# Swapping the rotary channel halves with DMAs inside SBUF instead of a TensorE permutation, and turning at the end of each block's VectorE list

## The chip, the cores and the metric

One Trainium2 chip, of which the kernel uses one core. The metric is the device time in microseconds (us) of one execution of the whole program. Engines are named as in the profile: PE is TensorE, DVE is VectorE, ACT is ScalarE, POOL is GpSimd, SP is SyncE.

## What is computed

Two layers of a hybrid mixer on 256 latent and 256 context tokens of width 2048. Each layer has one input projection whose columns form a convolution branch, a two-directional gated recurrence, and windowed attention with 8 query and 2 key heads of 128 channels; then one output projection. The latent queries and keys get a two-dimensional rotary turn before attention:

```
def _rotate_half(t):
    t1, t2 = jnp.split(t, 2, axis=-1)
    return jnp.concatenate([-t2, t1], axis=-1)

def apply_axial_rope(x, cos, sin):
    xf = x.astype(jnp.float32)
    xr, xc = jnp.split(xf, 2, axis=-1)
    xrot = jnp.concatenate([_rotate_half(xr), _rotate_half(xc)], axis=-1)
    return (xf * cos[:, None, :] + xrot * sin[:, None, :]).astype(x.dtype)
```

So with the 128 channels of a head on the partitions, the four groups of 32 channels change places in pairs (0 with 1, 2 with 3), and the first of each pair gets a minus. That is done for 10 tiles of 128 channels x 256 tokens a layer (2 k, 8 q), 20 in all.

## The kernel before

Channels lie on the 128 partitions, tokens in the free dimension. A layer is a list of blocks of 128 output columns each (`BLOCKS`, 56 a layer: x, k, v, the convolution's inputs, then q 0-3, their gates, q 4-7, their gates, two further gate groups, 16 output blocks). The program's l counts the layers from 0; this text says layer 1 (l = 0) and layer 2 (l = 1). A block's weights (1 MB) are split into a high and a low fp32r part: ACT copies the high half (`hi`), DVE subtracts for the low (`lo`), in two halves of 8 tiles each, and PE does three products per tile (L614 to L616), 16 tiles a block. In layer 1 a block streams 512 columns, in layer 2 most blocks stream only 256.

Everything around these products is written out as a table of steps: step b of an engine's loop does block b's part and the side work tied to b. The order on each engine is the order in the code:

- PE, step b: `mm_half(b, 0)`; transposes of the modulation rows (`ada_tp`, L509) and P times V (`pv`) where they fall due; `mm_half(b, 1)`; `rope_mm`; value transposes; recurrence gates (`lru_mm`, L648); attention scores (L669); probability transposes (`p_tp`, L682); modulation products (`ada_mm`, L501).
- ACT, step b: `hi` of the block two ahead, each half after PE has finished with the buffer (that is the halves of block b); the block's copy out of PSUM (`evac`, L875 for q); square roots and tanh of the recurrence; the rest of attention; `ada_rows` (L813), which copies modulation sums into `adasb`, the same memory as `lnr`, and first waits for the latest turn.
- DVE, step b: `lo` of the block two ahead (L1077), `evac`, `rope`, the running maximum of the softmax (L1299), the recurrence's scans and taps (L1249 to L1234), the convolution's taps (L1272, L1276: `CONV_TAPS`), `att_norm` (L1309, L1311).
- POOL has ten memsets and nothing else. SP issues all DMAs.

The rotary turn of block r stands in step `ROPE_AT[l]`: step 9 and 10 for k of layer 1, 13 and 14 for k of layer 2, and in both layers steps 17 to 20 for q 0-3 (blocks 16 to 19) and 25 to 28 for q 4-7 (blocks 24 to 27). PE multiplies a signed permutation matrix (`perm`, fp32) with the tile (L627); DVE multiplies the PSUM result with sine into `lnr` (L1211), the tile with cosine in place (L1212), and adds (L1214). `misc` lists who holds the PSUM bank `psM`: the next user on PE waits for the last (`misc_free`), so a `rope_mm` waits until DVE has read the one before.

Who waits for a turn: `scores` of each layer's first group (step 22) for the second k and q 3; the first group of the second key head for q 7 (step 30 in layer 1, step 29 in layer 2: `LAST_GROUPS`); `ada_rows` in steps 14 and 27 of layer 1.

```
ROPE_AT = [{9: 4, 10: 5, 17: 16, 18: 17, 19: 18, 20: 19, 25: 24, 26: 25, 27: 26, 28: 27},
           {13: 12, 14: 13, 17: 16, 18: 17, 19: 18, 20: 19, 25: 24, 26: 25, 27: 26, 28: 27}]
```

Of the kernel before, what the change touches and what calls it, by code (L numbers as in the profile page):

```python
# [21 lines left out]
ALU = mybir.AluOpType  # L22
AX = mybir.AxisListType

P = 128
D = 2048
DT = D // P
LAT, CTX = 256, 256
# [9 lines left out]
CT = 4  # L38
EPS = 1e-6
ADA_KINDS = 3  # L40
SHIFT, SCL, GATE = range(3)
# [10 lines left out]
BLOCKS = [[("x", t) for t in range(CT)] + first + REST for first in (KV + GLU, GLU + KV)]  # L52
# [159 lines left out]
def program(nc, io, known):  # L212
    ctx = ExitStack()
    with ctx:
# [180 lines left out]
        def conv_taps(l, b):  # L395

            plan = CONV_TAPS[l]
            assert sum(plan) == TAPS * CT // 2
            if not 0 <= b - CONV_AT[l] < len(plan):
                return []  # L400
            first = sum(plan[:b - CONV_AT[l]])
            return [(2 * (n // TAPS) + i, n % TAPS) for n in range(first, first + plan[b - CONV_AT[l]]) for i in range(2)]

        block = ctx.enter_context(nc.Block())

# [64 lines left out]

        @block.gpsimd
        def _(pool):
            nc.gpsimd.memset(cstat[:, :, :], 0.0).then_inc(*C.up("cstat_zero"))
            nc.gpsimd.memset(eps[:, :], EPS).then_inc(*C.up("eps_set"))
            nc.gpsimd.memset(bd[:, :, :, :], 0.0).then_inc(*C.up("bd_zero"))
            for l in range(LAYERS):
                if l:
                    pool.wait_ge(*C.at("scores", l - 1, max(groups(l - 1))))
                else:  # L480
                    pool.wait_ge(*used(last_of(NRAW + 1)))
                    pool.wait_ge(*used(last_of(NRAW + 2)))
                nc.gpsimd.memset(lrux[:, :, :, :], 0.0).then_inc(*C.up("lrux_zero", l))
                if l == 0:
                    pool.wait_ge(*used(last_of(NRAW)))
                    nc.gpsimd.memset(glu[:, :, :, :], 0.0).then_inc(*C.up("glu_zero"))

        @block.tensor
        def _(pe):  # L490
# [105 lines left out]
            def mm_half(gb, j):  # L596
# [18 lines left out]
                    mm(ps[:, 0:n], hi, hl[:, k, t], start=False, stop=False)  # L615
                    last = mm(ps[:, 0:n], lo, hh[:, k, t], start=False, stop=(at == DT - 1))  # L616
                last.then_inc(*C.up("mm", u))

            def rope_mm(l, b):

                kind, i = BLOCKS[l][b]
                if not misc:
                    pe.wait_ge(*C.at("evac_act", OPEN[0] - 1))
                pe.wait_ge(*C.at("evac_act", l * NB + b))
                misc_free(l)
                src = kT[:, i, 0:LAT] if kind == "k" else q[:, i, 0:LAT]
                mm(psM[:, 0:LAT], perm, src, start=True, stop=True).then_inc(*C.up("rope_mm", l, kind, i))  # L627

            def misc_free(l):

                if misc:
                    pe.wait_ge(*C.at(*misc[-1]))
# [105 lines left out]
            for gb in range(GLOB):  # L738
                l, b = divmod(gb, NB)
                if b == 0:  # L740
                    scores_free.clear()
                    if l:
                        rms_mm(l)
                        for a in PLAN[NB]:
                            ada_mm(*a)
                        for quarter in range(4):
                            for pair in range(SIDE // 2):
                                mm_quarter(quarter, pair)
                    else:
                        for c in range(CHUNKS):  # L750
                            mm_chunk(c)
                if b < OPEN[l]:
                    continue
                mm_half(gb, 0)

                for a in done_before(l, b):
                    ada_tp(*a)
                if b - TP_LAG[l] - 1 in groups(l):
                    pv(l, b - TP_LAG[l] - 1)
                mm_half(gb, 1)  # L760

                if b in ROPE_AT[l]:
                    rope_mm(l, ROPE_AT[l][b])
                    misc.append(("rope_t", l, *BLOCKS[l][ROPE_AT[l][b]]))
                if b and BLOCKS[l][b - 1][0] == "v":
                    i = BLOCKS[l][b - 1][1]
                    pe.wait_ge(*C.at("evac_act", gb - 1))
                    misc_free(l)
                    for kt in range(4):
                        last = nc.tensor.transpose(psM[:, kt * P:(kt + 1) * P], tbuf[:, kt * P:(kt + 1) * P], ident)  # L770
                    last.then_inc(*C.up("v_tp", l, i))
                    misc.append(("v_out", l, i))
                if b in LRU_MM[l]:
                    lru_mm(l, LRU_MM[l].index(b))
                if b in groups(l):
                    scores(l, b)
                if b - TP_LAG[l] in groups(l):
                    p_tp(l, b - TP_LAG[l])
                if b == LN_SUM[l]:
                    ln_mm(l, "ln_sum")  # L780
                if b == LN_VAR[l]:
                    ln_mm(l, "ln_var")
                if b == PW_AT:
                    for m in range(CT):
                        pw_mm(l, m)
                    misc.append(("pw_out", l, CT - 1))
                if l == 0:
                    for a in PLAN[b]:
                        ada_mm(*a)
# [271 lines left out]
        def _(dve):  # L1061
# [142 lines left out]
            def rope(l, b):  # L1204

                kind, i = BLOCKS[l][b]
                x = kT[:, i, 0:LAT] if kind == "k" else q[:, i, 0:LAT]
                dve.wait_ge(*C.at("rope_mm", l, kind, i))
                if (l, kind, i) != (0, "k", 0):
                    dve.wait_ge(*C.ago("rope"))  # L1210
                V.tensor_tensor(lnr[:, 0:LAT], psM[:, 0:LAT], sin, ALU.mult).then_inc(*C.up("rope_t", l, kind, i))  # L1211
                V.tensor_tensor(x, x, cos, ALU.mult).then_inc(*C.up("rope_c", l, kind, i))  # L1212
                dve.wait_ge(*C.ago("rope_c"))
                V.tensor_tensor(x, x, lnr[:, 0:LAT], ALU.add).then_inc(*C.up("rope", l, kind, i))  # L1214

            def taps(l, t):

# [118 lines left out]
            for dst, src, f in ((s4, tiny[:, 2, 0:n], 4.0), (s4n, tiny[:, 2, 0:n], -4.0), (dwh, at["dw_w"], 0.5),  # L1336
                                (hbr, at["b_r"], 0.5), (hbi, at["b_i"], 0.5), (lnhg, at["ln_g"], 0.5),
                                (lnhb, at["ln_b"], 0.5), (nsink, sink, -1.0)):
                V.tensor_scalar(dst, src, f, None, ALU.mult).then_inc(*C.up("derived"))
            dve.wait_ge(*C.ago("derived"))  # L1340

            for m in range(DT - 1):
                rms_add(0, m)
            for gb in range(GLOB):
# [28 lines left out]
                if gb + 2 < GLOB and b < NB - 1:  # L1373
                    lo(unit(0, gb + 2, 1))
                evac(gb)
                if b in ROPE_AT[l]:
                    rope(l, ROPE_AT[l][b])
                if b in groups(l):
                    att_max(l, b)
                if b in LRU_MM[l]:  # L1380
# [3 lines left out]
                if b in LRU_TAPS[l]:  # L1384
                    taps(l, LRU_TAPS[l].index(b))
                conv(l, conv_taps(l, b))
                if b in groups(l):
                    att_norm(l, b)
                if b == LN_SUM[l] - 1:
# [104 lines left out]
```

## Time and profile before

| | |
|---|---|
| time, median of 3 runs | 1322.59 us (1319.38 to 1323.63) |
| the profiled execution: time | 1322.9 us |
| its span in the trace | 1321.1 us, at a mean granted PE clock of 0.99 |
| PE busy | 1258.6 us (95%) |
| DVE busy | 733.7 us (56%) |
| ACT busy | 534.6 us (40%) |
| POOL busy | 8.2 us (1%) |
| HBM read | 230.54 MB, 176 GB/s over the span |

The busy time of an engine says how much work it has, not whether that work sets the end. For that the chain of waits is read, and then the stretch itself in the timeline: start, duration, engine, line, and in brackets how long the engine sat idle before it and what released it. PE's matmuls are pipelined, so the durations in the timeline overlap; what one costs is seen from start to start.

### The profile page before, as it was taken

How to read it: one execution, taken by the hardware profiler on the slowest of the kernel's cores; microseconds unless marked ns; L12 is line 12 of the kernel's file. 1: busy time of each engine (PE TensorE's matmuls, PEld its weight loads, DVE VectorE, ACT ScalarE, POOL GpSimd, SP SyncE). 2: the span in 40 equal slices, each digit the busy share in tenths (PEclk: the TensorE clock that was granted, in tenths of full speed). 3: DMA queues.
4: the chain of work that ended last, by engine and by line, in shares of the span. 5: the costliest groups of instructions: out<-in, count | busy, mean ns of one | idle time of the engine just before them, and what ended most of it. 6: DMA issues, size and time to landing. Idle time of an engine off the chain costs nothing.

```text
span 1321.1 us, 17033 instructions
## 1 busy us (share of the span) xinstructions
PE 1258.6 (95%) x7004; PEld 970.9 (73%) x7004; DVE 733.7 (56%) x1188; ACT 534.6 (40%) x843; POOL 8.2 (1%) x10
## 2 busy tenths in 40 slices
PE   3798999999999999999999999989999999999996
PEld 1465777767777777776777777758887998889995
DVE  3443436687565555552343233385789976755554
ACT  5222344452223334453332122244665554565452
POOL 0000100000000000000000000000000000000000
PEclk9999999999999999999999999989999999999998
DMA  9999655446443333333454554453332433325541
GB/s 343 332 320 324 220 201 212 191 192 263 155 187 128 128 127 127 128 128 134 169 225 175 213 208 173 186 191 104 120 131 93 160 128 128 128 96 192 182 169 64
DMA packets 76317, 233.73 MB, mean 177 GB/s; under 512 B 8016, under 2 KB 50128, under 8 KB 54352
## 3 DMA queue, kind: packets, MB, share of 16 engines
q1 hardware_dynamic: 76240, 232.65, 49.0%
q8 instruction: 55, 0.90, 0.3%
q14 instruction: 22, 0.18, 0.0%
HBM read 230.54 MB, written 2.10 MB: 176 GB/s over the span
## 4 chain that ended last, share of the span: by engine, by line
PE 83%; DVE 7%; DMA 5%; ACT 3%; issue 1%; SPq 0%; DVEq 0%; ACTq 0%
PE psum_block L614 21%; PE psum_block L615 20%; PE psum_block L616 20%; PE psum_ada L501 5%; PE psum_scores L691 3%; PE psum_scores L648 2%; PE psum_scores L669 2%; DMA raw<-in_w_ada 2%; DVE w_lo L1077 2%; DMA Y<-in_xT 1%; PE psum_scores L682 1%; DMA qreg<-in_w_ada 1%; DVE T L1128 1%; DVE h_lo L1135 1%; DMA glu<-in_w_ada 1%
## 5 line engine op out<-in xcount | busy, mean ns | idle before, releaser
L614 PE MATMUL psum_block<-h_hi,w_hi 128*128 128x512 f32 (+1 forms) x1616 | 562.4, 348 | 0.7 <-ACT glu L1050 0.7
L615 PE MATMUL psum_block<-h_lo,w_hi 128*128 128x512 f32 (+1 forms) x1616 | 547.9, 339 | 0.0
L616 PE MATMUL psum_block<-h_hi,w_lo 128*128 128x512 f32 (+1 forms) x1616 | 547.7, 339 | 0.0
L1077 DVE TENSOR_TENSOR w_lo<-raw,w_hi 128x1024 fp32r<-128x1024 f32 x218 | 263.4, 1218 | 398.6 <-ACT w_hi L803 398.4
L803 ACT ACTIVATE w_hi<-raw 128x1024 fp32r<-128x1024 f32 x218 | 228.5, 1053 | 530.1 <-PE psum_block L616 516.2
L614 PEld LDWEIGHTS psum_block<-h_hi,w_hi 128*128 128x128 f32 x1616 | 306.3, 190 | 78.1 <-issue 38.7
L615 PEld LDWEIGHTS psum_block<-h_lo,w_hi 128*128 128x128 f32 x1616 | 306.6, 190 | 35.3 <-issue 3.8
L616 PEld LDWEIGHTS psum_block<-h_hi,w_lo 128*128 128x128 f32 x1616 | 306.4, 190 | 34.2
L1276 DVE SCALAR_TENSOR_TENSOR Y<-glu,small,Y 128x512 f32<-128x512 f32 (+1 forms) x240 | 130.4, 612 | 0.0
L501 PE MATMUL psum_ada<-raw,cstat 128*32 128x512 f32 x512 | 67.2, 616 | 5.4 <-DMA raw<-in_w_ada 5.4
L917 ACT ACTIVATE T<-psum_scores,stats 128x512 f32<-128x512 f32 (+1 forms) x48 | 28.9, 615 | 52.7 <-DVE stats L1301 52.7
L844 ACT ACTIVATE h_hi<-T,ada 128x256 fp32r<-128x256 f32 x64 | 28.7, 501 | 45.4 <-DVE T L1128 45.4
L1085 DVE TENSOR_REDUCE tiny<-psum_ada 128x4 f32<-128x16 f32 x16 | 2.0, 169 | 71.3 <-PE psum_ada L531 71.3
L523 PE MATMUL psum_ada<-raw,cstat 128*32 128x256 f32 x272 | 20.5, 424 | 21.1 <-DMA raw<-in_w_ada 21.1
L691 PE MATMUL psum_scores<-T,v 128*128 128x512 f32 x80 | 36.4, 593 | 1.4 <-ACT T L932 1.4
L501 PEld LDWEIGHTS psum_ada<-raw,cstat 128*32 128x32 f32 x512 | 11.5, 109 | 34.5 <-issue 26.5
L831 ACT ACTIVATE T<-Y 128x512 f32<-128x512 f32 (+1 forms) x48 | 26.1, 550 | 22.4 <-DVE Y L1201 13.3
L648 PE MATMUL psum_scores<-T,bd 128*128 128x512 f32 x64 | 30.7, 625 | 3.9 <-DVE T L1234 3.9
L923 ACT ACTIVATE T<-T,stats 128x512 f32<-128x512 f32 (+1 forms) x48 | 27.3, 640 | 13.6 <-DVE stats L1311 13.6
L1234 DVE SCALAR_TENSOR_TENSOR T<-qreg,small,T 128x512 f32<-128x512 f32 x48 | 32.5, 745 | 0.0
L523 PEld LDWEIGHTS psum_ada<-raw,cstat 128*32 128x32 f32 x272 | 7.7, 118 | 32.5 <-issue 16.1
L669 PE MATMUL psum_scores<-kT,qreg 128*128 128x512 f32 x64 | 31.4, 611 | 0.0
(174 smaller groups left out, 1105.6 us busy)
## 6 DMA issues: line engine op xcount, KB each, us to landing
raw<-in_w_blocks SPq DMA_DIRECT2D x105, 1024.0 KB, 4.8
raw<-in_w_ada SPq DMA_DIRECT2D x81, 1024.0 KB, 5.5
qreg<-in_w_ada SPq DMA_DIRECT2D x10, 1024.0 KB, 11.2
glu<-in_w_ada SPq DMA_DIRECT2D x5, 1024.0 KB, 9.7
Y<-in_xT SPq DMA_DIRECT2D x4, 1024.0 KB, 12.4
T<-in_xT SPq DMA_DIRECT2D x16, 256.0 KB, 7.2
raw<-in_w_blocks SPq DMA_DIRECT2D x4, 896.0 KB, 11.4
raw<-in_pw SPq DMA_DIRECT2D x2, 1024.0 KB, 6.2
```

The source lines that it names most:

```text
L501: last = mm(psA[32 * j:32 * j + 32, :], cstat[:, k, 2:34], w[:, j * TOK:(j + 1) * TOK], start=(k == 0), stop=(k == DT - 1), tile_position= ...
L614: mm(ps[:, 0:n], hi, hh[:, k, t], start=(at == 0), stop=False)
L615: mm(ps[:, 0:n], hi, hl[:, k, t], start=False, stop=False)
L616: last = mm(ps[:, 0:n], lo, hh[:, k, t], start=False, stop=(at == DT - 1))
L648: last = mm(psS[:, 2 * d + g, :], bd[:, g, d * CT + t, :], T[:, 4 * d, :], start=True, stop=True)
L669: mm(psS[:, g, :], qt, kT[:, kv, :], start=True, stop=False)
L691: last = mm(psS[:, 0, :], v[:, kt, kv * HD:(kv + 1) * HD], T[:, 4 + kt, :], start=(kt == first), stop=(kt == 3))
L803: fn(wh[:, u % 4, 0:cols.stop - cols.start], raw_of(item)[:, cols], ACT.Copy).then_inc(*C.up("hi", u))
L917: fn(T[:, g, k0:TOK], psS[:, g, k0:TOK], ACT.Exp, scale=SCALE, bias=st[:, 1, g:g + 1], accum_out=st[:, 2, g:g + 1]).then_inc(*C.up("att_ex ...
L1077: V.tensor_tensor(wl[:, u % 4, 0:n], raw_of(item)[:, cols], wh[:, u % 4, 0:n].bitcast(F32), ALU.subtract).then_inc(*C.up("lo", u))
L1234: stt(out, x, lcw[:, c, k:k + 1], out, ALU.mult, ALU.add).then_inc(*C.up("taps", l, t, d))
L1276: stt(out, x, dwh[:, c:c + 1], out, ALU.mult, ALU.add).then_inc(*C.up("conv", l, t, k))
```

## The change

The permutation matmul goes. In its place POOL issues four DMAs for each turn, from SBUF to SBUF, 32 partitions of 1 KB each, that lay the tile's groups of 32 channels swapped into one of two halves of `lnr`. Each set of four waits for the tile's copy out of PSUM, and for the turn two before (whose half of `lnr` it uses); in layer 1 also for the modulation transposes that read `adasb`. DVE then multiplies the swapped copy with sine in place. The minus sign moves into the sine table: two small DVE instructions at the start of the program (the row sums of `perm`, and a scaling of `sin`). In DVE's list of a step, `rope` moves from ahead of the softmax maximum, recurrence and convolution to behind the convolution, ahead of `att_norm`. The users of `psM` no longer wait for turns.

```
+        def rope_of(l, b):
+            kind, i = BLOCKS[l][b]
+            return kT[:, i, 0:LAT] if kind == "k" else q[:, i, 0:LAT]
+
+        def turned_of(l, b):
+
+            n = list(ROPE_AT[l].values()).index(b) % 2
+            return lnr[:, n * LAT:(n + 1) * LAT]
...
         @block.gpsimd
         def _(pool):
+            def turn(l, s, b):
+
+                kind, i = BLOCKS[l][b]
+                order = list(ROPE_AT[l].values())
+                n = order.index(b)
+                pool.wait_ge(*C.at("evac_act", l * NB + b))
+                if n >= 2:
+                    pool.wait_ge(*C.at("rope", l, *BLOCKS[l][order[n - 2]]))
+                elif l:
+                    pool.wait_ge(*C.at("ln_n", 0, CT - 1))
+                    pool.wait_ge(*C.at("ada_tp", 1, GATE))
+                if l == 0:
+                    for step, items in PLAN.items():
+                        for rows in items:
+                            if step < s and rows[2] == DT - 1:
+                                pool.wait_ge(*C.at("ada_tp", *rows[:2]))
+                for quad in range(0, P, 32):
+                    nc.gpsimd.dma_start(turned_of(l, b)[quad:quad + 32, :], rope_of(l, b)[quad ^ 32:(quad ^ 32) + 32, :]
+                                        ).then_inc(*C.up(f"turned{n % 2}", l, kind, i, quad, by=16))
+
...
+                for s, b in ROPE_AT[l].items():
+                    turn(l, s, b)
...
-            def rope_mm(l, b):
-
-                kind, i = BLOCKS[l][b]
-                if not misc:
-                    pe.wait_ge(*C.at("evac_act", OPEN[0] - 1))
-                pe.wait_ge(*C.at("evac_act", l * NB + b))
-                misc_free(l)
-                src = kT[:, i, 0:LAT] if kind == "k" else q[:, i, 0:LAT]
-                mm(psM[:, 0:LAT], perm, src, start=True, stop=True).then_inc(*C.up("rope_mm", l, kind, i))
-
...
-                if b in ROPE_AT[l]:
-                    rope_mm(l, ROPE_AT[l][b])
-                    misc.append(("rope_t", l, *BLOCKS[l][ROPE_AT[l][b]]))
...
-                dve.wait_ge(*C.at("rope_mm", l, kind, i))
-                if (l, kind, i) != (0, "k", 0):
-                    dve.wait_ge(*C.ago("rope"))
-                V.tensor_tensor(lnr[:, 0:LAT], psM[:, 0:LAT], sin, ALU.mult).then_inc(*C.up("rope_t", l, kind, i))
+                x = rope_of(l, b)
+                turned = turned_of(l, b)
+                n = list(ROPE_AT[l].values()).index(b)
+                dve.wait_ge(*C.at(f"turned{n % 2}", l, kind, i, P - 32))
+                V.tensor_tensor(turned, turned, sin, ALU.mult).then_inc(*C.up("rope_t", l, kind, i))
                 V.tensor_tensor(x, x, cos, ALU.mult).then_inc(*C.up("rope_c", l, kind, i))
+                dve.wait_ge(*C.ago("rope_t"))
                 dve.wait_ge(*C.ago("rope_c"))
-                V.tensor_tensor(x, x, lnr[:, 0:LAT], ALU.add).then_inc(*C.up("rope", l, kind, i))
+                V.tensor_tensor(x, x, turned, ALU.add).then_inc(*C.up("rope", l, kind, i))
...
+            V.tensor_reduce(st[:, 0, 0:1], perm, axis=AX.X, op=ALU.add).then_inc(*C.up("derived"))
+            dve.wait_ge(*C.ago("derived"))
+            V.tensor_scalar(sin, sin, st[:, 0, 0:1], -1.0, ALU.mult, ALU.mult).then_inc(*C.up("derived"))
...
                 evac(gb)
-                if b in ROPE_AT[l]:
-                    rope(l, ROPE_AT[l][b])
                 if b in groups(l):
                     att_max(l, b)
...
                 conv(l, conv_taps(l, b))
+                if b in ROPE_AT[l]:
+                    rope(l, ROPE_AT[l][b])
                 if b in groups(l):
                     att_norm(l, b)
```

The line numbers of the changed kernel are about 20 higher: L1077 becomes L1095, L1180 L1198, the turn's L1211, L1212, L1214 become L1229, L1230, L1233, the convolution's L1276 becomes L1295, and the scores' L669 L690.

DVE, layer 2, steps 27 and 28, from `lo` of the block two ahead on. Before:

```order
L1077 TENSOR_TENSOR w_lo<-raw,w_hi 128x1024 x2
L1211 TENSOR_TENSOR lnr<-psum_misc,small 128x256
L1212 TENSOR_TENSOR qreg<-qreg,small 128x256
L1214 TENSOR_TENSOR qreg<-qreg,lnr 128x256
L1276 SCALAR_TENSOR_TENSOR Y<-glu,small,Y 128x256 x6
L1077 TENSOR_TENSOR w_lo<-raw,w_hi 128x1024
L1318 SCALAR_TENSOR_TENSOR Y<-psum_scores,Y 128x4x128
L1077 TENSOR_TENSOR w_lo<-raw,w_hi 128x1024
L1180 SCALAR_TENSOR_TENSOR Y<-Y,psum_block 128x256
L1211 TENSOR_TENSOR lnr<-psum_misc,small 128x256
L1212 TENSOR_TENSOR qreg<-qreg,small 128x256
L1214 TENSOR_TENSOR qreg<-qreg,lnr 128x256
```

The same place with the change:

```order
L1095 TENSOR_TENSOR w_lo<-raw,w_hi 128x1024 x2
L1295 SCALAR_TENSOR_TENSOR Y<-glu,small,Y 128x256 x6
L1229 TENSOR_TENSOR lnr<-lnr,small 128x256
L1230 TENSOR_TENSOR qreg<-qreg,small 128x256
L1233 TENSOR_TENSOR qreg<-qreg,lnr 128x256
L1095 TENSOR_TENSOR w_lo<-raw,w_hi 128x1024
L1337 SCALAR_TENSOR_TENSOR Y<-psum_scores,Y 128x4x128
L1095 TENSOR_TENSOR w_lo<-raw,w_hi 128x1024
L1198 SCALAR_TENSOR_TENSOR Y<-Y,psum_block 128x256
L1295 SCALAR_TENSOR_TENSOR Y<-glu,small,Y 128x256 x6
L1229 TENSOR_TENSOR lnr<-lnr,small 128x256
L1230 TENSOR_TENSOR qreg<-qreg,small 128x256
```

The turn of a step now stands behind the six convolution taps of that step instead of ahead of them, and reads `lnr`, not PSUM.

POOL, the end of its list in layer 1 and in layer 2 (four of the DMAs make one turn):

```order
L500 DMA lnr<-kT 32x256 x8
L500 DMA lnr<-qreg 32x256 x32
L512 MEMSET qreg 128x2096
L500 DMA lnr<-kT 32x256 x8
L500 DMA lnr<-qreg 32x256 x32
```

Before, the one MEMSET was POOL's only instruction there; now 40 DMAs stand in its queue ahead of it and 40 behind it, in program order.

## Rows read from the trace of the kernel before

**Rows 1.** The page, parts 1 and 4: busy time; chain that ended last
```profile
PE 1258.6 (95%) x7004; PEld 970.9 (73%) x7004; DVE 733.7 (56%) x1188; ACT 534.6 (40%) x843; POOL 8.2 (1%) x10
...
PE 83%; DVE 7%; DMA 5%; ACT 3%; issue 1%; SPq 0%; DVEq 0%; ACTq 0%
```

**Rows 2.** PE timeline, layer 2, end of step 28: start us, us, engine, line
```profile
1121.89 0.28 PE L616 MATMUL psum_block<-h_hi,w_lo 128*128 128x256 f32 x1
1122.01 0.59 PE L627 MATMUL psum_misc<-qreg,small 128*128 128x256 f32 x2
1122.25 0.47 PE L614 MATMUL psum_block<-h_hi,w_hi 128*128 128x256 f32 x1
1122.56 0.28 PE L615 MATMUL psum_block<-h_lo,w_hi 128*128 128x256 f32 x1
1122.67 0.28 PE L616 MATMUL psum_block<-h_hi,w_lo 128*128 128x256 f32 x1
```

**Rows 3.** PE timeline, layer 1: a step with a turn, and one without
```profile
320.24 0.39 PE L616 MATMUL psum_block<-h_hi,w_lo 128*128 128x512 f32 x1
320.47 0.59 PE L627 MATMUL psum_misc<-qreg,small 128*128 128x256 f32 x2
320.99 0.64 PE L501 MATMUL psum_ada<-raw,cstat 128*32 128x512 f32 x4
...
371.37 0.39 PE L616 MATMUL psum_block<-h_hi,w_lo 128*128 128x512 f32 x1
371.69 0.64 PE L501 MATMUL psum_ada<-raw,cstat 128*32 128x512 f32 x4
```

**Rows 4.** PE's waits, whole span: line, releaser, us in total, times, longest
```profile
PE psum_scores L648 <- DVE T L1234: 3.9, 2, 2.8
...
PE psum_misc L627 <- DVE lnr L1211: 0.3, 1, 0.3
```

**Rows 5.** Timelines of ACT, DVE and PE, layer 2, steps 13 and 14
```profile
1000.33 1.15 ACT L908 ACTIVATE qreg<-qreg 128x512 f32<-128x512 f32 x2
...
1001.00 1.29 DVE L1249 TENSOR_TENSOR T<-T,qreg 128x512 f32<-128x512 f32 x2
...
1006.14 4.06 DVE L1234 SCALAR_TENSOR_TENSOR T<-qreg,small,T 128x512 f32<-128x512 f32 x6
...
1010.25 1.13 PE L648 MATMUL psum_scores<-T,bd 128*128 128x512 f32 x2 [1.09 <-DVE T L1234]
```

**Rows 6.** Timelines of DVE, ACT and PE, layer 1, steps 27 and 28
```profile
467.50 0.42 DVE L1211 TENSOR_TENSOR lnr<-psum_misc,small 128x256 f32<-128x256 f32 x1
...
468.28 0.43 DVE L1214 TENSOR_TENSOR qreg<-qreg,lnr 128x256 f32<-128x256 f32 x1
468.62 4.06 DVE L1276 SCALAR_TENSOR_TENSOR Y<-glu,small,Y 128x512 f32<-128x512 f32 x6
...
468.80 0.60 ACT L813 ACTIVATE lnr<-psum_ada 128x512 f32<-128x512 f32 x1 [0.90 <-DVE qreg L1214]
...
473.02 0.60 PE L509 MATMUL psum_ada<-rounded,lnr 128*128 128x128 f32 x4
```

**Rows 7.** DVE: `lo` in the page's part 5; timeline, layer 2, step 25
```profile
L1077 DVE TENSOR_TENSOR w_lo<-raw,w_hi 128x1024 fp32r<-128x1024 f32 x218 | 263.4, 1218 | 398.6 <-ACT w_hi L803 398.4
...
1103.77 0.16 DVE L1309 TENSOR_TENSOR stats<-stats 128x4 f32<-128x4 f32 x1 [1.96 <-ACT stats L920]
```

**Rows 8.** Timelines of DVE and PE, layer 2, steps 28 and 29
```profile
1124.83 0.42 DVE L1211 TENSOR_TENSOR lnr<-psum_misc,small 128x256 f32<-128x256 f32 x1
...
1125.62 0.42 DVE L1214 TENSOR_TENSOR qreg<-qreg,lnr 128x256 f32<-128x256 f32 x1
1125.96 2.46 DVE L1276 SCALAR_TENSOR_TENSOR Y<-glu,small,Y 128x256 f32<-128x256 f32 x6
...
1128.19 1.02 PE L669 MATMUL psum_scores<-kT,qreg 128*128 128x512 f32 x2
```

**Rows 9.** DVE timeline, start of the program
```profile
7.98 0.31 DVE L1339 TENSOR_SCALAR der<-small 128x8 f32<-128x8 f32 x3
13.80 5.47 DVE L1108 TENSOR_TENSOR T<-T 128x512 f32<-128x512 f32 x7 [5.51 <-ACT T L831]
```

**Rows 10.** Timelines, layer 2: copies of q 0 and q 6; first scores
```profile
1033.47 0.38 ACT L875 ACTIVATE qreg<-psum_block 128x256 f32<-128x256 f32 x1 [1.27 <-DVE Y L1263]
...
1067.56 1.02 PE L669 MATMUL psum_scores<-kT,qreg 128*128 128x512 f32 x2
...
1108.55 0.36 ACT L875 ACTIVATE qreg<-psum_block 128x256 f32<-128x256 f32 x1
```

**Rows 11.** DMA issues by line: count, KB each, median us to landing; SP timeline
```profile
raw<-in_w_blocks SPq DMA_DIRECT2D x105, 1024.0 KB, 4.8
...
out<-Y SPq DMA_DIRECT2D x4, 512.0 KB, 3.7
...
822.40 0.33 SPq L454 DMA_DIRECT2D raw<-in_w_ada  x1
822.77 0.43 SPq L454 DMA_DIRECT2D raw<-in_w_blocks  x1
```

More of the change, by code:

```diff
@@ L1206, in rope @@
                 kind, i = BLOCKS[l][b]
-                x = kT[:, i, 0:LAT] if kind == "k" else q[:, i, 0:LAT]
-                dve.wait_ge(*C.at("rope_mm", l, kind, i))
-                if (l, kind, i) != (0, "k", 0):
-                    dve.wait_ge(*C.ago("rope"))
-                V.tensor_tensor(lnr[:, 0:LAT], psM[:, 0:LAT], sin, ALU.mult).then_inc(*C.up("rope_t", l, kind, i))
+                x = rope_of(l, b)
[3 more added lines that the diff above has]
+                V.tensor_tensor(turned, turned, sin, ALU.mult).then_inc(*C.up("rope_t", l, kind, i))
                 V.tensor_tensor(x, x, cos, ALU.mult).then_inc(*C.up("rope_c", l, kind, i))
+                dve.wait_ge(*C.ago("rope_t"))
                 dve.wait_ge(*C.ago("rope_c"))
-                V.tensor_tensor(x, x, lnr[:, 0:LAT], ALU.add).then_inc(*C.up("rope", l, kind, i))
+                V.tensor_tensor(x, x, turned, ALU.add).then_inc(*C.up("rope", l, kind, i))
             def taps(l, t):
```

## The prediction

> **What bounds the kernel now.** I read the page first: PE is busy 95% of the span, and the chain that ended last runs 83% over PE and 7% over DVE [rows 1]. So an instruction taken off PE is worth its time unless the place it stood in was a wait for something else. Next the list of PE's waits, for such places behind the turns: two waits for the recurrence's taps, 3.9 us in all, and one of a `rope_mm` for DVE, 0.3 us [rows 4]. Then the timelines around the 20 turns, where I looked for three things: what a turn costs PE, who waits for its result, and how much time lies between the copy of q or k out of PSUM and the place where DVE now wants the swapped copy.
>
> **What PE gives up.** One turn is two fp32 passes of 256 columns. In layer 2, from the last product ahead of the turn to the second product behind it is 1122.56 - 1121.89 = 0.67 us; without the turn it would be two starts of 0.12 us (1122.01 - 1121.89), so the turn costs 0.43 [rows 2]. In layer 1 a step with a turn takes 320.99 - 320.24 = 0.75 us from product to modulation, one without 0.32: again 0.43 [rows 3]. Twenty turns: -8.6 us. The 0.3 us wait for DVE [rows 4] goes too, since the bank is no longer shared with the turns: -0.3.
>
> **What is eaten at once.** At 1010.25 PE waits 1.09 us for the taps of layer 2's last recurrence tile [rows 5]. Their chain starts on ACT (square roots at 1000.33, the first over when DVE begins L1249 at 1001.00) and runs on DVE without a gap to 1010.20. The turn ahead of it on DVE ends just as ACT delivers, so moving it away brings the chain no earlier. The two turns of steps 13 and 14 therefore buy PE only a longer wait: +0.9 of the 8.6.
>
> **What the new place on DVE costs.** It hides nearly everywhere: the three instructions are as long as before, 1.2 us from 467.50 to 468.71 [rows 6], and ahead of `lo` DVE sits idle for 398 us in all until ACT delivers [rows 7]. Two consumers are close. First, `ada_rows` in step 27 of layer 1 waits for the turn of q 6. Behind six taps the turn starts at 467.50 + 4.06 = 471.56 and ends at 472.77; ACT follows 0.1 later and copies 0.6; PE could start L509 at 473.5. It wants it at 473.02 - 0.43 = 472.6 [rows 6]. New wait: +0.9. Second, layer 2's scores in step 29 want q 7, turned in step 28. The taps move up to 1124.83 and end at 1127.3, the turn at 1128.5; PE wants the scores at 1128.19 - 0.43 = 1127.76 and gets them at 1128.6 [rows 8]: +0.8. (Both sides of each difference hang on the end of the same product, so earlier savings shift them together.) The softmax normalization behind the turn in step 25 of layer 2 stays covered: DVE waits 1.96 us there for ACT's exponentials, and the turn of 1.2 fits in [rows 7]. The two added instructions at the start lie in a DVE gap of 5.5 us [rows 9]: nothing, and if they were late, their own length (three of their neighbours take 0.31).
>
> **What the swap costs.** The trace of before has no POOL-issued DMA and none inside SBUF, so it is bounded from rows. A swap is four DMAs of 32 KB. From below: SP gets rid of one in 0.33 to 0.43 us without waiting for it to land [rows 11]. From above: one DMA at a time. 512 KB land in 3.7 us, 1024 KB in 4.8; the 512 KB between them are worth 1.1, so the fixed part is 2.6, and 32 KB make it 2.7 [rows 11]. Traffic itself is nothing: 80 x 32 KB = 2.6 MB beside 230 MB.
>
> How long may a DMA take in POOL's queue (call it d) before someone waits? The tight stretch is q 0-3 of layer 2, where a block is 48 products of 0.12 us and a turn, 6.2 us [rows 2]. q 0 is copied at 1033.85, the scores want q 3 turned at 1067.56 - 4 x 0.43 = 1065.8, less 1.3 for DVE's turn and handing over [rows 10]. That leaves 30.7 us for 16 DMAs, d = 1.92. The second is q 6 and 7: from 1108.91 to where DVE wants q 7's copy, 1127.3 [rows 8, 10]: 18.3 us for 8 DMAs, d = 2.29. In layer 1 the blocks are twice as long and nothing is close. Below d = 1.92 the swaps cost nothing, since what runs on DVE up to its turn covers them; above it PE pays 16 us per microsecond of d, above 2.29 24 us. I take d under 1.92: queued DMAs on SP are issued every 0.4 us, and a source and destination inside SBUF should not be slower than the rows from HBM. Both ends stay in the range: 0 and, at d = 2.7, 16 x 0.78 + 8 x 0.41 = 15.8 us.
>
> [...]
>
> **The sum.** -8.6 - 0.3 + 0.9 + 0.9 + 0.8 = -6.3 us. The profiled execution took 1322.9 us (span 1321.1 and 1.8 around it), 0.3 above the median: **1316.6 us**, 0.5% faster. A measurement of this kernel tells a change from none from about 0.3% (4 us) on.
>
> **The rivals.**
>
> *One DMA at a time from POOL.* POOL can't pass a DMA on until the one before has landed, and d reaches 2.7. Then q 3 comes 12.5 us late and q 7 3.3 us: 1316.6 + 15.8 = **1332.4**, slower. It decides from d = 2.31 on, where 16 x 0.39 + a little eats the 6.3. Chance 0.33, of which a part lies so low in d that the result is within 0.3%.
>
> *The gain is mostly absorbed.* The steps with attention in layer 2 (25 to 28) run so close between PE, ACT and DVE that the four turns there and the 0.3 give nothing: -6.3 + 1.7 + 0.3 = -4.3. With two more new waits of 0.9, the size of the two I found, that is -2.5, **1320.4**. For it: the 0.3 us wait and one of the two new ones are in these steps. Against it: in PE's list no other turn waits. Chance 0.12. [...]
>
> *Neither new wait appears*, since a row's duration overlaps the next one's start and DVE's lists are shorter than I add up: 1322.9 - 8.9 + 0.9 = **1314.9**. Chance 0.08.
>
> **How the numbers follow.** The forecast has 0.47, the three rivals 0.33, 0.12 and 0.08. Faster by over 0.3%, that is under 1318.6: of the forecast 0.39 (2 us of further loss would miss it, which I give 0.08) and the last rival's 0.08, together 0.47. Within 0.3%: those 0.08, the absorbed case's 0.12 less the little of it that ends faster or slower, and the low end of the first rival, some 0.05: 0.24. Slower: the rest, 0.29. The range starts at 1313, below the last rival by the spread of runs, and must reach past 1332.4 to leave no more than 2 in 10 out: 1334. The forecast's own range is 1313 to 1319.
>
> **What would show it.** No L627 on PE; POOL's 80 DMAs in the queue table. If right: the wait for the taps at about 1008 grows from 1.1 to about 1.9 us; a new wait of about 0.9 at the modulation transposes in step 28 of layer 1 and of 0.8 at layer 2's scores of step 29; DVE's L1229 never idle long before it. If the first rival holds: DVE idle before L1229 on a DMA in steps 18 to 20 of layer 2, growing from turn to turn, PE waiting for `lo` or for the scores of step 22, and four POOL DMAs spaced over 2 us apart. In layer 1 the swaps should be hidden either way; a wait there would show that d is over 3 us and my bounds wrong.

## The result and the profile after

The changed kernel takes 1348.99 us (median of 4 runs, 1347.27 to 1349.56) against 1321.46 us for the kernel before, run beside it. The ratio is 1.0206 (95% interval 1.0187 to 1.0225): 2.1% slower, where 0.5% faster was forecast, and above the range's end of 1334. The profiled execution has a span of 1346.9 us, 25.8 more than before's.

The page of the kernel after, parts 1 and 4, answers to [rows 1]:

```profile
PE 1262.9 (94%) x6964; PEld 970.8 (72%) x6964; DVE 734.4 (55%) x1190; ACT 534.1 (40%) x843; POOL 49.0 (4%) x90
...
PE 75%; DVE 10%; DMA 5%; issue 5%; ACT 4%; POOL 1%; SPq 0%; DVEq 0%; ACTq 0%; POOLq 0%
```

PE runs 40 instructions fewer, as planned, and is busy 4.3 us *longer*. The chain has moved from PE to DVE, POOL and "issue". The list of waits, which answers to [rows 4], says for what (all releasers, whole span; line numbers have moved: L648 is now L669, L669 is L690, L614 to L616 are L645 to L647, L1077 is L1095, L1211 is L1229, L1214 is L1233):

```profile
DVE lnr L1229 <- DMA lnr<-qreg: 31.5, 6, 7.3
PE psum_scores L690 <- DVE qreg L1233: 10.1, 2, 8.3
PE psum_block L645 <- DVE w_lo L1095: 6.7, 3, 4.6
PE psum_scores L669 <- DVE T L1253: 4.8, 2, 2.8
PE psum_block L645 <- DVE Y L1198: 4.5, 2, 3.9
```

DVE waits 31.5 us for the swapped copies, in six turns, all of them in layer 2 (q 0 to 3, 6 and 7). PE then waits for what is queued behind the turn on DVE, `lo` and a block's eviction, and for the turned q itself. POOL's timeline in layer 2, q 0 to q 3 (start, duration, idle ahead of it), gives the cause:

```profile
1032.68 0.50 POOL L500 DMA_DIRECT2D lnr<-qreg  x1 [27.02 <-ACT qreg L893]
1034.66 0.51 POOL L500 DMA_DIRECT2D lnr<-qreg  x1 [1.48 <-issue]
1036.68 0.51 POOL L500 DMA_DIRECT2D lnr<-qreg  x1 [1.51 <-issue]
1041.86 0.50 POOL L500 DMA_DIRECT2D lnr<-qreg  x1 [4.67 <-issue]
...
1071.54 0.51 POOL L500 DMA_DIRECT2D lnr<-qreg  x1 [1.51 <-issue]
1077.53 0.50 POOL L500 DMA_DIRECT2D lnr<-qreg  x1 [5.48 <-issue]
```

An issue keeps POOL 0.5 us, and yet no two stand closer than 2.0 us. Between some there are 4.4 to 6.0. "issue" as the releaser says only that POOL waited for nothing the profile can name. Sixteen DMAs need 15 intervals for 1077.53 - 1032.68 = 44.85 us, 2.99 us each, where 1.92 was allowed.

The same turns on DVE, and what they do to PE:

```profile
1056.56 0.42 DVE L1229 TENSOR_TENSOR lnr<-lnr,small 128x256 f32<-128x256 f32 x1 [4.83 <-DMA lnr<-qreg]
...
1079.22 0.42 DVE L1229 TENSOR_TENSOR lnr<-lnr,small 128x256 f32<-128x256 f32 x1 [7.27 <-DMA lnr<-qreg]
```
```profile
1059.04 0.58 PE L645 MATMUL psum_block<-h_hi,w_hi 128*128 128x256 f32 x1 [4.60 <-DVE w_lo L1095]
...
1151.16 1.19 PE L690 MATMUL psum_scores<-kT,qreg 128*128 128x512 f32 x1 [8.27 <-DVE qreg L1233]
```

Idle time is not all. Windows of PE from the recurrence's last products of layer 2 to the scores of its last attention group, before and then after (length, busy PE, PEld, DVE, ACT, POOL, granted clock, DMA share, GB/s):

```profile
1010.25:1155.40 145.15, 144.65 (x1007) 128.37 (x1008) 116.60 (x212) 76.87 (x125) 0.00 (x0) 1.00 0.37 131
```
```profile
1005.85:1181.10 175.25, 152.82 (x990) 132.14 (x991) 117.65 (x215) 76.04 (x124) 16.16 (x32) 0.92 0.33 115
```

The stretch grows by 30.1 us: 21.9 of idle PE (22.43 against 0.50) and 8.2 of busy PE, at a granted clock of 0.92 instead of 1.00, although the stretch holds eight turns fewer (q 0 to 7). Narrower windows show that the clock falls just behind the idle times:

```profile
1055.00:1060.00 5.00, 0.96 (x4) 0.96 (x5) 3.34 (x5) 2.26 (x3) 1.34 (x3) 0.76 0.06 17
1060.00:1065.00 5.00, 5.00 (x28) 5.00 (x27) 1.70 (x5) 0.38 (x1) 0.51 (x1) 0.56 0.67 219
1065.00:1070.00 5.00, 2.39 (x20) 2.18 (x19) 2.63 (x5) 2.01 (x3) 1.48 (x3) 1.00 0.05 13
```

Up to 1005.85 the kernel was 4.4 us *ahead* of before; at layer 2's first scores it is 13.0 behind, at the last group 25.7, and there it stays to the end. The whole loss lies in these 175 us.

### The profile page after: what moved, and what is told of

Its sections match the earlier page's. It is cut to its first block, busy times and chain, and to the rows that moved or that the text cites. A ratio compares the mean times of both kernels' runs of the same rounds, so it can differ in the third digit from the quotient of the medians.

```text
span 1346.9 us, 17035 instructions
## 1 busy us (share of the span) xinstructions
PE 1262.9 (94%) x6964; PEld 970.8 (72%) x6964; DVE 734.4 (55%) x1190; ACT 534.1 (40%) x843; POOL 49.0 (4%) x90
## 4 chain that ended last, share of the span: by engine, by line
PE 75%; DVE 10%; DMA 5%; issue 5%; ACT 4%; POOL 1%; SPq 0%; DVEq 0%; ACTq 0%; POOLq 0%
PE psum_block L645 18%; PE psum_block L646 18%; PE psum_block L647 18%; PE psum_ada L532 4%; PE psum_scores L669 2%; DVE w_lo L1095 2%; PE psum_scores L690 2%; PE psum_scores L712 2%; DMA raw<-in_w_ada 2%; DVE Y L1295 1%; DMA Y<-in_xT 1%; DMA qreg<-in_w_ada 1%; DMA glu<-in_w_ada 1%; ACT T L935 1%; ACT w_hi L821 1%
## 5 line engine op out<-in xcount | busy, mean ns | idle before, releaser
L645 PE MATMUL psum_block<-h_hi,w_hi 128*128 128x512 f32 (+1 forms) x1616 | 563.3, 349 | 11.8 <-DVE w_lo L1095 6.7
L647 PE MATMUL psum_block<-h_hi,w_lo 128*128 128x512 f32 (+1 forms) x1616 | 549.3, 340 | 0.0
L1095 DVE TENSOR_TENSOR w_lo<-raw,w_hi 128x1024 fp32r<-128x1024 f32 x218 | 263.0, 1218 | 387.0 <-ACT w_hi L821 386.8
L645 PEld LDWEIGHTS psum_block<-h_hi,w_hi 128*128 128x128 f32 x1616 | 308.3, 191 | 89.8 <-issue 39.4
L647 PEld LDWEIGHTS psum_block<-h_hi,w_lo 128*128 128x128 f32 x1616 | 308.3, 191 | 34.2
L1295 DVE SCALAR_TENSOR_TENSOR Y<-glu,small,Y 128x512 f32<-128x512 f32 (+1 forms) x240 | 130.4, 612 | 0.0
L862 ACT ACTIVATE h_hi<-T,ada 128x256 fp32r<-128x256 f32 x64 | 28.7, 501 | 46.2 <-DVE T L1146 46.2
L500 POOL DMA_DIRECT2D lnr<-qreg x64 | 32.3, 505 | 398.7 <-ACT qreg L893 242.2
L690 PE MATMUL psum_scores<-kT,qreg 128*128 128x512 f32 x64 | 36.0, 686 | 11.0 <-DVE qreg L1233 10.1
L669 PE MATMUL psum_scores<-T,bd 128*128 128x512 f32 x64 | 32.4, 654 | 4.8 <-DVE T L1253 4.8
L532 PEld LDWEIGHTS psum_ada<-raw,cstat 128*32 128x32 f32 x512 | 11.5, 109 | 34.7 <-issue 26.6
```

Source lines behind the costliest of these rows:

```text
L532: last = mm(psA[32 * j:32 * j + 32, :], cstat[:, k, 2:34], w[:, j * TOK:(j + 1) * TOK], start=(k == 0), stop=(k == DT - 1), tile_position= ...
L645: mm(ps[:, 0:n], hi, hh[:, k, t], start=(at == 0), stop=False)
L669: last = mm(psS[:, 2 * d + g, :], bd[:, g, d * CT + t, :], T[:, 4 * d, :], start=True, stop=True)
L690: mm(psS[:, g, :], qt, kT[:, kv, :], start=True, stop=False)
L1095: V.tensor_tensor(wl[:, u % 4, 0:n], raw_of(item)[:, cols], wh[:, u % 4, 0:n].bitcast(F32), ALU.subtract).then_inc(*C.up("lo", u))
L1295: stt(out, x, dwh[:, c:c + 1], out, ALU.mult, ALU.add).then_inc(*C.up("conv", l, t, k))
```

## The experiments

### No swap at all

```diff
-                for s, b in ROPE_AT[l].items():
-                    turn(l, s, b)
...
-                V.tensor_tensor(turned, turned, sin, ALU.mult)
+                V.tensor_tensor(turned, x, sin, ALU.mult)
```

> Left out: the 64 swap DMAs; VectorE multiplies the unswapped channels by the sine table instead, so queries and keys get a wrong rotation; every other instruction stays where the change puts it. Waiting theory (the 25 us come from VectorE waiting for the swap's landings in the second layer): 1316 us (1322.9 - 8.9 for TensorE's products + 0.9 + 0.9 + 0.8 for the three small waits), and the waits of 4.4 to 7.3 us at VectorE's first rotation instruction are gone. Place theory (rotation behind the block's convolution taps makes releases late by itself): over 1335.

1318.14 us (10 runs), ratio 0.9978 (0.9964 to 0.9992). No DVE wait at the rotation is left. The loss is the waiting for the swap, and not the place; 31 us hang on it. (The expectation counts 64 swap DMAs, and so do two later ones. There are 80: 64 for q, 16 for k.) It is 2 us above the expected 1316, which the last experiment takes up.

### More descriptor memory

```diff
-... num_devices=1, dynamic_dma_scratch_size=64)
+... num_devices=1, dynamic_dma_scratch_size=192)
```

> [...] Ring theory (each GpSimd DMA waits until the one before has landed, 1.7 us alone and about 5 us behind a weight load in flight): four DMAs are issued close together, 16 DMAs of q0 to q3 in the second layer take under 25 us instead of 45, time 1315 to 1319. [...]

1317.49 us (10 runs), 0.9977 (0.9959 to 0.9996). One number in the build call gives back all that leaving the swaps out does. POOL's timeline in layer 1, the first turns of q, with 64 bytes:

```profile
308.11 0.50 POOL L500 DMA_DIRECT2D lnr<-qreg  x1 [119.22 <-ACT qreg L893]
310.12 0.51 POOL L500 DMA_DIRECT2D lnr<-qreg  x1 [1.51 <-issue]
315.80 0.51 POOL L500 DMA_DIRECT2D lnr<-qreg  x1 [5.18 <-issue]
320.52 0.50 POOL L500 DMA_DIRECT2D lnr<-qreg  x1 [4.21 <-issue]
```

and with 192 bytes:

```profile
308.39 1.49 POOL L500 DMA_DIRECT2D lnr<-qreg  x3 [131.98 <-ACT qreg L893]
315.09 0.50 POOL L500 DMA_DIRECT2D lnr<-qreg  x1 [5.21 <-issue]
```

Three go out 0.5 us apart, not the expectation's four; the fourth waits 5.2 us. So GpSimd's own work is 0.5 us per DMA, and how many DMAs go out before it waits hangs on the bytes set aside. That ends the GpSimd theory, by which the issues would have stayed 2 to 5 us apart: DVE's instructions are the same in both. The trace also tells when a DMA lands. For the one issued at 310.12 with 64 bytes:

```profile
DMA to landing us min/median/max: 5.4/5.4/5.4
```

It lands at 315.50, and the next is issued at 315.80. None of after's 80 DMAs is issued sooner than 0.30 us behind the landing of the one before, and 71 of them stand at just that distance. With 128 bytes there are never more than two in flight, with 192 never more than three.

> Descriptor memory of 128 bytes. With 192 bytes three DMAs were issued 0.5 us apart and the fourth waited, with 64 bytes every one waited. Ring theory: at 128 two DMAs go out together, the third waits for a landing; 16 DMAs of q0 to q3 in the second layer take 25 to 35 us, time between the two: 1320 to 1332. If the memory had to hold a whole swap of four to be of use, 1345 or more.

With 128 bytes: 1316.21 us (6 runs), 0.9959 (0.9932 to 0.9986), faster than I expected. DMAs go in pairs:

```profile
1028.83 0.98 POOL L500 DMA_DIRECT2D lnr<-qreg  x2 [29.23 <-ACT qreg L893]
1031.35 1.00 POOL L500 DMA_DIRECT2D lnr<-qreg  x2 [1.53 <-issue]
1033.88 0.99 POOL L500 DMA_DIRECT2D lnr<-qreg  x2 [1.53 <-issue]
1038.33 0.98 POOL L500 DMA_DIRECT2D lnr<-qreg  x2 [3.46 <-issue]
...
1054.34 0.98 POOL L500 DMA_DIRECT2D lnr<-qreg  x2 [1.55 <-issue]
```

Seven intervals of pairs take 1054.34 - 1028.83 = 25.51 us, 3.64 us a pair or 1.8 us a DMA. That is under the 1.92 of the prediction, and DVE's waits for the swap fall from 31.5 to 4.9 us.

> Descriptor memory of 512 bytes (the small tile of the start was put into another one to make room): all four DMAs of a swap go out 0.5 us apart, and no wait of VectorE at its first rotation instruction is over 1 us. Ring theory: the time of the kernel without swaps, 1315 to 1318, less spread over the runs than with 192 bytes. If what is left at 192 bytes is the transfers' own time behind weight loads, the waits of 3 to 5 us stay and the time is as with 192 bytes, 1317 to 1320.

In this kernel and in the next one with 512 bytes the small tile shares memory with a tile in use, so modulation values are overwritten; the instructions are the same. 1317.73 us (7 runs), and DVE has no wait for the swap any more:

```profile
1036.18 1.97 POOL L500 DMA_DIRECT2D lnr<-qreg  x4 [1.54 <-ACT qreg L893]
```

So 64, 128 and 192 bytes let one, two and three such DMAs out. 512 bytes show no wait for room: in the other kernel with that size ("Which size is best"), the eight DMAs of the two k of layer 1 go out in 4.05 us, with up to seven in flight.

```profile
163.69 4.05 POOL L500 DMA_DIRECT2D lnr<-kT  x8 [16.84 <-ACT kT L877]
```

### The same DMAs from ScalarE's queue

```diff
-                pool.wait_ge(*C.at("evac_act", l * NB + b))
+                act.wait_ge(*C.at("evac_act", l * NB + b))
...
-                    nc.gpsimd.dma_start(turned_of(l, b)[quad:quad + 32, :], ...
+                    nc.scalar.dma_start(turned_of(l, b)[quad:quad + 32, :], ...
```

> The same 64 DMAs with the same waits, issued by ScalarE's queue: in the first layer behind the high parts of the step's weights, in the second layer right behind the block's eviction. Ring theory: no descriptor memory in the way, the four DMAs of a swap start within 1 us of each other, land some 2 us later alone and 5 us later behind a weight load; time 1314 to 1320. If instead the transfer itself through loaded DMA engines is what is slow (bandwidth theory), VectorE still waits several us at the first rotation instruction in the second layer and the time stays over 1335.

1331.44 us (4 runs), 1.0076 (1.0053 to 1.0100): between the two forecasts. DVE never waits for the swap, which ends the bandwidth theory: beside the same loads the transfers are in time when they may overlap (they land 1.8 to 5.6 us behind their issue, median 2.6). But the issues cost ScalarE itself. Its timeline and PE's waits:

```profile
1037.69 0.38 ACT L871 ACTIVATE qreg<-psum_block 128x256 f32<-128x256 f32 x1 [2.40 <-DVE Y L1284]
1038.10 2.44 ACTq L962 DMA_DIRECT2D lnr<-qreg  x4
1040.59 0.60 ACT L1033 ACTIVATE v<-psum_misc 128x512 f32<-128x512 f32 x1 [2.52 <-issue]
```
```profile
PE psum_scores L690 <- ACT T L928: 7.4, 3, 4.6
PE psum_scores L647 <- DVE T L1255: 7.3, 2, 4.5
```

Four issues take ScalarE's queue 2.44 to 3.11 us, for each of the 20 turns. Here they hold the next copy up by 2.52 us; in other places, as behind the four at 315.98 (2.46 us), ScalarE would have waited for PE anyway (its next copy starts at 321.32, released by PE). PE waits for the attention's exponentials (7.4 us, a wait that after's list doesn't have) and longer for the recurrence's taps (7.3 against 4.8). I had weighed the DMAs in the queues and not the time that their issue takes from a busy engine.

### Only the place, in the kernel before

```diff
-                if b in ROPE_AT[l]:
-                    rope(l, ROPE_AT[l][b])
                 if b in groups(l):
                     att_max(l, b)
...
                 conv(l, conv_taps(l, b))
+                if b in ROPE_AT[l]:
+                    rope(l, ROPE_AT[l][b])
```

> The kernel before (products with the permutation on TensorE), with nothing but VectorE's rotation moved behind the block's convolution taps. Waiting theory: the place costs only the small waits (two of 0.9 in the steps 13 and 14, 0.8 at the scores, some at the shared PSUM bank): 1323 to 1328. Place theory: 1340 to 1350, most of the loss.

1339.21 us (4 runs), 1.0137 (1.0117 to 1.0157): my number was wrong by 11 us, the place theory's was nearly right, and its reason is not. With the products still on PE, the shared bank `psM` ties PE to DVE:

```profile
1016.74 1.19 PE L627 MATMUL psum_misc<-kT,small 128*128 128x256 f32 x2 [8.28 <-DVE lnr L1211]
```

PE may not write the second k's product before DVE has read the first one's, and DVE now reads it behind all its taps (at 1016.17). Two more waits for the same bank, 2.6 and 1.9 us, bring these to 12.8 of the 17.8 us lost. Swaps that don't pass through that bank are what makes the late place free; taken alone it is no part that can be added to the rest. The kernel without swaps, with the rotation late too, stands at 1318.

> As the kernel with 512 bytes, and VectorE's rotation back at the place that it has in the kernel before, ahead of the scores' maxima. The small waits that the late place makes (0.9 + 0.8 us) go, but the swap has some 5 us less to land in: 1314 to 1317 if it lands within 5 us, 1320 to 1330 if VectorE waits for it at the front.

The other way round, swaps by DMA (512 bytes) and the rotation back in front: 1317.97 us (10 runs) against 1317.73 in the late place, no difference.

### Where the DMAs cost

The expectation counts 24 DMAs left out in layer 2. There are 40 (ten turns of four), all left out; layer 1's 40 stay.

```diff
-                for s, b in ROPE_AT[l].items():
+                for s, b in ROPE_AT[l].items() if l == 0 else ():
                     turn(l, s, b)
```

> The changed kernel with its 64 bytes, and the 24 swap DMAs of the second layer left out (VectorE multiplies the unswapped channels there; the rotation of the second layer is wrong). Ring theory with my reading of where it costs (nothing in the first layer, all in the second): 1317 to 1319, as without any swap. If the first layer's 40 DMAs cost too, over 1325.

1319.42 us (7 runs), 0.9981 (0.9961 to 1.0001). Layer 1's 40 DMAs, one at a time with gaps of up to 5.8 us, cost at most the 1.3 us by which this is above the kernel without any, within the spread of either.

### The weight loads made small

```diff
+                if item[0] == "w" and item[1] >= NB + 8:
+                    dst, src = dst[:, 0:512], src[:, 0:512]
                 sp.dma_start(dst, src).then_inc(C.sem(f"raw{SLOT[i]}"), 16)
```

> The changed kernel with its 64 bytes and all 64 swap DMAs, but from the ninth block of the second layer on each block's weight load brings 256 KB instead of 1 MB (the rest of the slot keeps old weights, so the output is wrong). Every wait and instruction stays. Ring theory with the swap's landing slow only behind a weight load in flight: the issues stand 2.0 us apart nearly everywhere in the second layer, 16 DMAs of q0 to q3 take 30 to 36 us, time 1316 to 1322. [...]

1328.43 us (8 runs), 1.0050 (1.0031 to 1.0070): 20.6 of after's 27.5 us go. POOL's timeline:

```profile
1036.61 0.50 POOL L502 DMA_DIRECT2D lnr<-qreg  x1 [31.14 <-ACT qreg L895]
1038.60 0.51 POOL L502 DMA_DIRECT2D lnr<-qreg  x1 [1.48 <-issue]
1040.61 0.51 POOL L502 DMA_DIRECT2D lnr<-qreg  x1 [1.51 <-issue]
1043.45 0.50 POOL L502 DMA_DIRECT2D lnr<-qreg  x1 [2.32 <-issue]
...
1071.28 0.50 POOL L502 DMA_DIRECT2D lnr<-qreg  x1 [3.44 <-issue]
```

Still one at a time, but 34.67 us for 15 intervals, 2.31 each instead of 2.99. So the long intervals are the load's. The time stays over the 1316 to 1322 expected because 2.31 is still over 1.92: DVE waits 13.0 us in all, the four turns of q 0 to 3 growing from 1.2 to 5.2 us, and from the taps wait to the first scores it is 1075.14 - 1009.78 = 65.36 us, 8.1 more than before's 57.31. The prediction's formula, 16 x (2.31 - 1.92), gives 6.2; I should have used it here. (The kernel without swaps takes 58.49 us for this stretch, so 6.9 of the 8.1 are the swaps'.)

### Which size is best

> Descriptor memory of 512 bytes again, with the small tile laid into v, which is first written after the tile is last read (in the kernel of the earlier run it was laid into a tile that is in use then, so the values were overwritten). Same times as there: 1316 to 1319, four DMAs of a swap 0.5 us apart, no wait of VectorE for the swap over 1 us.

> The kernel with 128 bytes again, beside 512 bytes on the same chip: if the two differ by less than their intervals (1316 to 1318 both), what counts is only that no DMA waits alone for the one before; if 128 is slower by over 2 us, the third and fourth DMA of a swap still cost.

> 128 bytes and the rotation back ahead of the scores' maxima. With 512 bytes this place made no difference (1318.0 and 1317.7). With 128 bytes a swap takes some 3 us more from first issue to last landing: 1315 to 1319 if that still ends before VectorE comes to it, 1320 to 1326 if VectorE waits there.

On one chip, against the same runs of before: 512 bytes 1319.42 (12 runs), 0.9984 (0.9969 to 1.0000); 128 bytes 1315.83 (12 runs), **0.9957 (0.9942 to 0.9973)**; 128 bytes with the rotation in front 1317.29 (12 runs), 0.9963 (0.9948 to 0.9978). In this last one DVE does wait for the swap, 9.9 us in four turns, and the time still lies in the range expected for no wait. The change with 128 bytes beats both kernels, after by 33 us and before by 0.4%. That 512 is slower than 128 is not the swap's doing in the two profiled executions. From the first recurrence product of layer 1 to the last tile's in layer 2 they take 998.70 - 181.12 = 817.6 us (128) and 1004.58 - 186.32 = 818.3 (512), before 821.7; the 5.2 us between them arise ahead of that, in the opening, where PE waits for weights (22.8 us for 128 and 25.3 for 512) and the clock fell to 0.89 for 512 and stayed at 1.00 for 128. Windows of 128, then 512 bytes:

```profile
30.00:60.00 30.00, 22.87 (x198) 13.53 (x186) 15.59 (x37) 7.64 (x14) 0.00 (x0) 1.00 0.97 328
```
```profile
30.00:60.00 30.00, 24.65 (x191) 14.17 (x184) 15.60 (x37) 7.83 (x15) 0.00 (x0) 0.89 1.05 333
```

The first swap is issued at 158.49 us in the one and at 163.69 us in the other. Whether the medians of the two differ for that reason too isn't shown; the opening also varies between executions of one kernel.

### The term left out: the clock behind the taps

> The kernel with 128 bytes, with one product of the size of a turn (permutation times cosine table, its result unused) put back on TensorE in steps 13 and 14 of the second layer. Clock reading: in the runs without these two turns TensorE idles 2.0 us for the taps and its granted clock then falls to 0.53 to 0.56 for 3 us, before it idled 1.1 and kept 1.00; so with the two products the wait is again 1.1 us, the clock stays at 1.00 behind it, and the next marker (first scores of the second layer) stands 1.5 us earlier after the taps wait than in the 128-byte kernel: the two products cost nothing. If the clock fell for another reason, it falls here too. The time itself moves by less than these runs can tell: 1313 to 1318.

```diff
+                if l and b in (13, 14):
+                    misc_free(l)
+                    mm(psM[:, 0:LAT], perm, cos, start=True, stop=True).then_inc(*C.up("fill"))
```

The eight products at L669, with 128 bytes, and then with the two fillers:

```profile
998.70 5.40 PE L669 MATMUL psum_scores<-T,bd 128*128 128x512 f32 x8 [1.99 <-DVE T L1253]
```
```profile
1003.51 3.70 PE L669 MATMUL psum_scores<-T,bd 128*128 128x512 f32 x8 [1.08 <-DVE T L1256]
```

Windows around them, 128 bytes and fillers:

```profile
998.00:1001.00 3.00, 2.30 (x3) 0.97 (x4) 3.00 (x8) 1.63 (x2) 0.00 (x0) 0.67 0.00 0
```
```profile
1003.00:1006.00 3.00, 2.49 (x6) 1.25 (x7) 3.00 (x8) 1.92 (x3) 0.00 (x0) 1.00 0.00 0
```

In this pair, 0.9 us more of idling goes with 5.40 us for the eight products instead of 3.70, and with the two useless products back they are as fast as before. From there to the first scores it is 59.75 us without and 57.88 with them. But the profiled execution of the other run with 128 bytes, the same kernel without fillers, has this row:

```profile
1003.50 3.70 PE L669 MATMUL psum_scores<-T,bd 128*128 128x512 f32 x8 [1.99 <-DVE T L1253]
```

The same wait of 1.99 us stands ahead of the products, the clock behind it is 1.00, and the first scores follow after 1061.34 - 1003.50 = 57.84 us, as soon as with the fillers. In all, eleven profiled executions have this wait of 2.0 us (after's, and every experiment's but those with ScalarE's queue, with the place alone and with the fillers). In ten of them the products take 5.40 us (granted clock 0.55 to 0.67 over the first 3 us), in this one 3.70. Behind a wait of 1.1 us (before, and the fillers) they took 3.70 both times. So the slow clock is frequent behind the longer wait and not bound to it, and one execution with fillers doesn't show that they prevent it. The time, 1316.81 us (10 runs), 0.9964 (0.9947 to 0.9980), can't tell it, as expected.

## Why the prediction was wrong

**The step that failed** is the choice of d, the time of one DMA in POOL's queue: "I take d under 1.92: queued DMAs on SP are issued every 0.4 us". SP's queue was the wrong neighbour. d is 2.99 us over q 0 to 3 and 3.0 over q 6 and 7 (eight DMAs from 1125.70 to 1149.77), because with 64 bytes one DMA is out at a time and the next waits for its landing. The rival "one DMA at a time" was the case, with its mechanism, place and order of events: DVE waiting at L1229 for q 0 to 3 (4.85, 4.83, 5.57 and 7.27 us), PE idle for `lo`, then for the scores. Its 1332.4 was still 17 us too low. I gave this case 0.33, since no row of before showed such a limit; but no row showed its absence either, and the four separate DMAs in one queue and the 64 bytes were in the code.

**The bound was wrong too.** d = 2.7 came from single DMAs to or from HBM on SP's queue. In after's q 0 to 3 of layer 2, a swap's DMA issued with nothing else in flight has d = 2.0, with 1.7 us from issue to landing; issued behind a weight load still in flight it has a d of 4.4 to 6.0. The DMA issued at 310.12 in layer 1 made room only at 315.80. Meanwhile 1 MB loads ran (window of after):

```profile
311.00:315.00 4.00, 4.00 (x19) 3.32 (x18) 1.68 (x4) 1.06 (x1) 0.00 (x0) 1.00 1.01 416
```

"Traffic itself is nothing" held for bytes (2.6 MB) and failed for latency: that DMA landed after 5.4 us, where those issued with nothing else in flight took 1.7.

**The formula held, the clock was missing.** 16 x (2.99 - 1.92) = 17.1 us to the first scores. Measured: from 4.4 ahead to 13.0 behind, and four turns (1.7) that should have put it further ahead: 19.1. The kernel without swaps tells how much of this is the swaps': it takes 58.49 us from the taps wait to the first scores, after takes 1080.61 - 1005.85 = 74.76, which makes 16.3. The other 2.9 are there without any swap; of them 1.7 are the slow clock behind the taps and 0.9 a wait for `lo`. For q 6 and 7 the formula gives 8 x (3.01 - 2.29) = 5.8; measured 6.6 from q 6's copy (16.3 behind) to the scores of step 29 (23.0), or 7.5 with the two turns saved on the way. There the time allowed was too long: without swaps DVE comes to q 7's turn 1122.12 - 1105.23 = 16.9 us behind q 6's copy, not 18.3, which allows 2.1 a DMA and gives 7.2. The remaining 3.3 and 2.7 us follow the waits of 1.84 and 8.27 us, in stretches in which windows of 5 us have the clock at 0.66, and 0.50 to 0.84. In the first, two further waits of PE, 0.9 and 0.6 us, have a part. Over the whole stretch PE is busy 8.2 us longer beside 21.9 us more of idling: its stalls cost more here than their length.

**Point by point.** *Twenty turns, -8.6.* Right as far as the taps wait: of the 4.4 us ahead there, 0.8 were there at layer 1's first recurrence product, ahead of any turn. The other 3.6 stand against a forecast of 10 x 0.43 less the 0.9 at `ada_rows`, 3.4, the two turns of steps 13 and 14 being eaten. *Taps wait, 1.1 to 1.9.* 1.99, right; but "buy PE only a longer wait" left out the clock: in this execution, as in nine others of eleven with that wait, the products behind it took 1.7 us longer. That the longer wait is the reason isn't shown. *`ada_rows` in step 27, +0.9.* Right:

```profile
469.20 0.66 PE L540 MATMUL psum_ada<-rounded,lnr 128*128 128x128 f32 x4 [0.76 <-ACT lnr L831]
```

*Scores in step 29, +0.8.* 0.73 in the kernel without swaps, right. *The late place hidden elsewhere.* Nearly: a wait of 0.9 for `lo` in layer 2 (at 1035.03 without swaps) was not foreseen. *Layer 1's swaps hidden.* Right. With both new terms the sum is 1316.6 + 1.7 + 0.9 = 1319.2 for a kernel whose swaps cost nothing; measured 1315.8 to 1319.4 over the ten runs of this sort. Their profiled executions alone reach layer 1's first recurrence product at anything from 181 to 188 us.

## What to carry over

Before GpSimd is given DMAs in a row, compare the descriptor memory of the build with the number of DMAs that are to be out at once; room for two instead of one was enough here (1315.83 us against 1348.99). When an upper bound for an unseen resource comes from another queue, don't choose the value from the cheaper end: ask whether the transfers overlap, since one at a time turns latency into throughput (here 2.99 us a DMA one at a time, 1.8 in pairs). A wait on TensorE can have a second price, the clock behind it (here 0.55 to 0.67 over 3 us in ten of eleven executions, 1.7 us on eight products): read the granted clock there before an instruction is taken off TensorE in front of a wait. And one profiled execution is not enough to judge such a price: two executions of the same kernel differed in it by 1.9 us.

## What was not expected of the hardware

- GpSimd's issue of a DMA takes 0.50 us; with 64 bytes for descriptors the next is issued 0.30 us behind the landing of the last (71 of 80), which is 2.0 us behind its issue with nothing else in flight, and 4.4 to 6.0 us behind it when a 1 MB load was in flight at the issue (q 0 to 3 of layer 2). With 64, 128 and 192 bytes one, two and three DMAs of 32 rows were out at most, with 512 bytes up to seven.
- With more out at once each lands later than with one (median from issue 1.7, 2.2, 3.4 and 3.1 us with 64, 128, 192 and 512 bytes), yet the group is through sooner: from the first issue to the last landing of q 0 to 3 of layer 2 it is 46.5, 28.7, 29.2 and 22.7 us.
- Behind a wait of 2.0 us TensorE's granted clock fell to 0.55 to 0.67 over the next 3 us in ten of eleven profiled executions, and the eight products there took 5.40 us instead of 3.70. Behind a wait of 1.1 us it stayed at 1.00 both times.
- Four DMA issues in a row on ScalarE's queue keep it 2.44 to 3.11 us.
